# A hybrid attention and mixture-of-experts step on one core: identity products before the last expert products, a new order of work in the second layer, and token rows that wait in PSUM

## What is computed

```python
for l in range(2):
    h = adaln(x, norm_mix[l], shift, scale)          # RMS norm, then scale and shift
    x = x + gate * (attention(h @ w_in[l]) @ w_out[l])
    h = adaln(x, norm_ffn[l], shift_f, scale_f)
    x = x + gate_f * moe(h)                          # 16 experts, top 2 of one group
# moe: scores = softmax(h @ w_router); two experts a token
#      hid = silu(h @ w_gate[e]) * (h @ w_up[e]);  out = sum_e gates[e] * (hid @ w_down[e])
```

## Time and profile before

| | us |
|---|---|
| median of 3 runs (lowest, highest) | 1244.72 (1243.37, 1246.33) |
| the profiled execution, its whole time | 1242.9 |
| its span, first to last instruction | 1241.1 |
| PE busy | 1164.1 |
| DVE busy | 279.8 |
| ACT busy | 187.7 |

### The profile page before, as it was taken

How to read it: one execution, slowest core, us unless ns; L and a number is a source line. 1 busy time by engine, 2 the same in 40 slices (tenths; PEclk the granted TensorE clock), 3 DMA queues, 4 the chain that set the end, 5 groups by cost and what they waited for, 6 DMA issues and landing times.

```text
span 1241.1 us, 13752 instructions
## 1 busy us (share of the span) xinstructions
PE 1164.1 (94%) x5533; PEld 515.1 (42%) x5533; DVE 279.8 (23%) x673; ACT 187.7 (15%) x441; POOL 56.4 (5%) x68
## 2 busy tenths in 40 slices
PE   4999999999988899899999999999999998989898
PEld 1445464443423233334344454753434434343333
DVE  1146533121010101021232354312021110202013
ACT  1224322010000000001021343210001100000010
POOL 0412000000000000000013020000000000000000
PEclk9999999999999999999999999999999999999999
DMA  9999999999999999999997559899999999999997
GB/s 375 383 383 375 414 423 429 424 431 427 429 427 427 429 429 428 429 427 429 420 392 259 203 196 397 339 391 413 426 428 428 428 428 428 428 430 428 427 425 296
DMA packets 60084, 494.18 MB, mean 398 GB/s; under 512 B 5490, under 2 KB 6658, under 8 KB 28420
## 3 DMA queue, kind: packets, MB, share of 16 engines
q1 hardware_dynamic: 56992, 485.88, 94.5%
q0 software_dynamic: 2864, 7.46, 1.9%
q10 hardware_dynamic: 180, 0.17, 0.0%
HBM read 490.72 MB, written 3.16 MB: 398 GB/s over the span
## 4 chain that ended last, share of the span: by engine, by line
PE 72%; DMA 24%; issue 2%; ACT 1%; SPq 1%; DVE 1%; POOL 0%; DVEq 0%
PE bank L1190 39%; PE bank L942 12%; DMA ring<-in_w_up 9%; DMA ring<-in_w_gate 7%; DMA ring<-in_w_down 6%; PE bank L952 3%; PE bank L1140 3%; PE bank L898 3%; PE bank L1151 3%; DMA ring<-in_w_in_ab 2%; PE bank L874 2%; PE bank L1216 1%; PE bank L959 1%; PE bank L997 1%; PE bank L1246 1%
## 5 line engine op out<-in xcount | busy, mean ns | idle before, releaser
L1190 PE MATMUL bank<-ring,hT 128*64 128x512 f32 x2520 | 574.3, 606 | 48.0 <-issue 20.1
L1190 PEld LDWEIGHTS bank<-ring,hT 128*64 128x64 f32 x2520 | 191.2, 139 | 401.6 <-issue 392.8
L942 PE MATMUL bank<-ring,hT 128*128 128x512 f32 x320 | 141.8, 600 | 3.1 <-DMA ring<-in_w_in_ab 2.4
L942 PEld LDWEIGHTS bank<-ring,hT 128*128 128x128 f32 x320 | 60.5, 192 | 79.9 <-issue 77.3
L1983 DVE TENSOR_TENSOR work<-work,bank 128x512 f32<-128x512 f32 x56 | 38.5, 688 | 164.0 <-PE bank L1151 163.8
L1976 DVE TENSOR_TENSOR work<-work,bank 128x512 f32<-128x512 f32 x32 | 22.0, 688 | 223.6 <-PE bank L1190 198.8
L1190 PE MATMUL bank<-work,hT 128*64 128x512 f32 x284 | 69.5, 593 | 0.0
L1140 PE MATMUL bank<-work 128*128 128x128 f32 x512 | 60.3, 275 | 0.0
L1140 PEld LDWEIGHTS bank<-work 128*128 128x128 f32 x512 | 58.7, 192 | 1.6 <-issue 1.6
L1519 ACT ACTIVATE hT<-bank 128x512 f32<-128x512 f32 x32 | 19.0, 595 | 256.9 <-PE bank L1246 256.9
L2024 DVE COPY work<-bank 128x512 f32<-128x512 f32 x14 | 9.7, 692 | 207.3 <-PE bank L1190 207.3
(11 more groups left out here) (220 smaller groups left out, 754.4 us busy)
## 6 DMA issues: line engine op xcount, KB each, us to landing
ring<-in_w_gate SPq DMA_DIRECT2D x56, 2048.0 KB, 17.7
ring<-in_w_up SPq DMA_DIRECT2D x50, 2048.0 KB, 17.2
ring<-in_w_down SPq DMA_DIRECT2D x46, 2048.0 KB, 17.0
ring<-in_w_mod SPq DMA_DIRECT2D x23, 2048.0 KB, 11.1
work<-in_w_up SPq DMA_DIRECT2D x8, 2048.0 KB, 15.2
ring<-in_w_down SPq DMA_DIRECT2D x14, 1024.0 KB, 14.7
ring<-in_w_in_c SPq DMA_DIRECT2D x6, 2048.0 KB, 21.1
ring<-in_w_in_ab SPq DMA_DIRECT2D x4, 2048.0 KB, 21.6
```

The source lines that it names most:

```text
L942: ins = pe.matmul(b[:, 0:n], hT[:, c, t * P:(t + 1) * P], w[:, c, 0:n], start=i == 0, stop=i == DC - 1)
L1190: ins = pe.matmul(bank[banks[j]][64 * e:64 * e + 64, :], lhs[:, 4 * h + c, 64 * e:64 * e + 64], weights(e, c, j), start=(h, c) == (0, 0), ...
```

## The change

It has these parts.

1. **Identity products.** In the last pair of each layer `rows_first` multiplies the four halves of `x` by the identity into the banks of the last scatter, four products of 128 x 512, after the down unit 8 and before unit 10. The last scatter adds to them. `add_last` on DVE is gone: in layer 0 DVE copies the four halves out (`rows_out`), and ACT squares the sample halves straight from PSUM; in layer 1 ACT copies all four.
2. **`shift_logits(1)`** moves from between the scatter products of layer 0 to just before `rows_first`.
3. **Order of DVE and of the first projection** at the start of layer 1: both gated halves of t = 0 come before the norm, whose request is split in two; the first projection of layer 1 begins with chunk 0 (ACT's) instead of chunk 4.
4. **Order of the dense units of layer 1**: `("in", 4, 0)` directly after `("in", 4, 1)`; `("mod", 1, 2, 0)` and `("in", 5, 1)` after the scores of batch 2; values wait only for the unit that they read.
5. **Token rows of layer 1**: the sample's transposes (`hk`, 1) no longer stand before the output projection, but one half after `xT` and one after `("hT", 1, 0)`. `keep_busy(2)` after `xT` and its wait go, `keep_busy(5)` becomes 2.
6. **Parked rows.** In layer 1 ACT copies the four halves of `x` to banks 4 to 7 before and during the first gather (`park`), and DVE copies them back after the last down product of pair 0. So in pair 0 the hidden transposes go to banks 0 and 3, the down products to 0 and 1, and the gather of pair 1 to 2 and 1. PE waits for the count job before the first gather.
7. **A megabyte into x.** `load_where_parked` loads row block 2 of the last down unit of pair 0, 0.5 MB for each expert, into `x`, once the rows are parked and before `load_halves(0, ...)`, which loses its two loads of 0.5 MB.

```diff
-        "scores": [("in", 4, 1), ("in", 5, 1)],
-        0: [("in", 4, 0)],
-        1: [("T", 0), ("mod", 1, 2, 0), ("in", 5, 0)],
+        "scores": [("in", 4, 1), ("in", 4, 0)],
+        0: [("mod", 1, 2, 0), ("in", 5, 1)],
+        1: [("T", 0), ("in", 5, 0)],
         2: [("mod", 1, 2, 1)],
         3: [("mod", 1, 2, 2)],
         4: [("wo", 0, 1)],
         5: [("wo", 1, 1)],
         (6,): [("mod", 1, 2, 3)],
         (7,): [("modT", 2)],
-        7: [("hT", 1, 1), ("wo", 0, 0), ("hk", 1), ("woh", 0), ("woh", 1), ("rt", 1), ("xT",),
-            ("rt", 0), ("hT", 1, 0), ("hk", 0), ("pos",)]}}
+        7: [("hT", 1, 1), ("wo", 0, 0), ("woh", 0), ("woh", 1), ("rt", 1), ("xT",), ("hkh", 1, 0),
+            ("rt", 0), ("hT", 1, 0), ("hkh", 1, 1), ("hk", 0), ("pos",)]}}
...
-                    for half in range(2):
+                    for half in range(2 if n else 1):
...
+                def load_where_parked(e):
+
+                    slot = moe_slot(l, ring_turn(0, MOE_UNITS - 2 + e))
+                    src = a["w_down"][l].rearrange("e k n -> (e k n)")[e * D * D:(e + 1) * D * D].rearrange("(h p r) -> h p r", h=2, p=P)[1]
+                    sp.wait_ge(m["parked"], 2 if e else 4)
+                    sp.wait_ge(moe_ld[l][slot], 16)
+                    sp.dma_start(x[:, e, :], src[:, 2 * D:3 * D]).then_inc(moe_ld[l][slot], 16)
...
                     load_quarter(1)
+                    load_where_parked(1)
+                    load_where_parked(0)
                     load_halves(0, MOE_UNITS - 2, 1)
                     load_halves(1, 0, 2)
...
-                    keep_busy(5)
+                    keep_busy(2)
...
-                    c = 4 * ((i + 1) % 2) + i // 2
+                    half = (i + 1 + l) % 2
+                    c = 4 * half + i // 2
...
-                if j % BATCHES == 0:
-                    pe.wait_ge(*emptied_by(("qkv", l, IN_UNITS[l] - 1, t)))
+                if l == 0 and j % BATCHES == 0:
+                    pe.wait_ge(*emptied_by(("qkv", 0, 4, t)))
+                elif l == 1 and b % 2 == 0:
+                    pe.wait_ge(*emptied_by(("qkv", 1, 4 + b // 2, t)))
...
-                if l == 1:
-                    pe.wait_ge(mod_emptied, 6)
-                    keep_busy(2)
...
+                    apart = bank[3] if l else bank_of(("hT", l, 1, 0, 0))
...
+                    if first and l:
+                        pe.wait_ge(*emptied_by(("count", 1)))
...
+                        if l == 1 and early and (n, k) == (0, SLOTS + 2) and j:
+                            pe.wait_ge(m["hg_ready"], 4)
+                        if l == 1 and early and (n, k) == (1, 0):
+                            pe.wait_ge(m[f"yd{j}_ready"], 1)
...
+                def rows_first(n):
+
+                    pe.wait_ge(m["y_added"], 4 * n + 5)
+                    for t in (1, 0):
+                        for h in range(2):
+                            pe.matmul(last_bank(t, h)[:, :], K("ident"), x[:, t, h * UC:(h + 1) * UC], start=True, stop=False)
+
                 def last_scatter():
 
                     for t in (1, 0):
                         for h in range(2):
                             pe.wait_ge(m["yd_gated"], 3 - 2 * t + h)
                             pe.matmul(last_bank(t, h)[:, :], GT[:, t, :], ydg[t][:, h * UC:(h + 1) * UC],
-                                      start=True, stop=True).then_inc(m["scattered"], 1)
-                        if (l, t) == (0, 1):
-                            shift_logits(1)
...
+                        if l == 0:
+                            shift_logits(1)
+                        rows_first(n)
                         last_product(n, 10, (6, 7), hidT, m["down_half"])
...
+                        down = (0, 1) if isinstance(n, int) and (l, n) == (1, 0) else (6, 7)
+                        product(n, 8, down, hidT, m["ht_ready"])
+                        product(n, 10, down, hidT, m["ht_ready"], m["down_half"])
...
+                def park(t, u):
+
+                    act.wait_ge(*emptied_by({(0, 0): ("hT", 1, 1, 0, 0), (0, 1): ("hT", 1, 1, 0, 1), (1, 0): ("hk", 1, 1, 1), (1, 1): ("hk", 1, 0, 0)}[t, u]))
+                    act.activation(bank[4 + 2 * t + u][:, :], x[:, t, u * UC:(u + 1) * UC], ACT.Copy).then_inc(m["parked"], 1)
...
+                if l:
+                    park(1, 0)
+                    park(1, 1)
+                    park(0, 0)
                 gathered(0)
...
+                end = more * PAIRS + PAIRS
+                if l == 0:
+                    for u in range(2):
+                        act.wait_ge(m["scattered"], 4 * end + u + 1)
+                        act.activation(xn(0, 1)[:, u * UC:(u + 1) * UC], last_bank(1, u)[:, :], ACT.Square,
+                                       accum_out=ss[:, 1 + 4 * u:2 + 4 * u]).then_inc(half_squares if u == 0 else ssq_ready, 1)
+                else:
+                    for t in (1, 0):
+                        for u in range(2):
+                            act.wait_ge(m["scattered"], 4 * end + 2 * (1 - t) + u + 1)
+                            act.activation(x[:, t, u * UC:(u + 1) * UC], last_bank(t, u)[:, :], ACT.Copy).then_inc(x_ready, 1)
...
+                    if first and l:
+                        dve.wait_ge(moe_used[l], used(0, 11))
+                        for t in (1, 0):
+                            for u in range(2):
+                                dve.tensor_copy(x[:, t, u * UC:(u + 1) * UC], bank[4 + 2 * t + u][:, :]).then_inc(m["y_added"], 1)
...
-                    add_last(end, 1, 0)
-                    add_last(end, 1, 1)
                     gate_down(0, 0)
-                    norm_asked(1, 0, 1)
                     gate_down(0, 1)
+                    first_half_scaled(1, 0, 1)
+                    rows_out(end, 1, 0)
+                    second_half_asked(1, 0, 1)
+                    rows_out(end, 1, 1)
+                    dve.wait_ge(x_ready, 4 + 2)
                     normed_rows(1, 0, 1)
-                    add_last(end, 0, 0)
+                    rows_out(end, 0, 0)
                     modulate(1, 0, 1)
-                    add_last(end, 0, 1)
+                    rows_out(end, 0, 1)
```

More of the change, by code:

```diff
@@ L1060, in logits, with token_rows @@
                     keep_busy(2)
-            def token_rows(l, t):
-                for h in range(2):
+            def token_rows(l, t, halves=(0, 1)):
+                for h in halves:
                     if (l, t, h) == (1, 0, 1):
@@ L1138, in gather @@
                                 at = (4 * h + c) * P
-                                to = bank_of(("hT", l, 1, 0, 0)) if first and h == 0 and c >= 2 else bank[2 if first and h else h]
+                                to = apart if first and h == 0 and c >= 2 else bank[2 if first and h or parked and not h else h]
                                 ins = pe.matmul(to[:, c * P:(c + 1) * P], htok(t)[:, at:at + P], pick[:, t, :],
@@ L1237, in last_scatter @@
                             pe.matmul(last_bank(t, h)[:, :], GT[:, t, :], ydg[t][:, h * UC:(h + 1) * UC],
-                                      start=True, stop=True).then_inc(m["scattered"], 1)
-                        if (l, t) == (0, 1):
-                            shift_logits(1)
+                                      start=False, stop=True).then_inc(m["scattered"], 1)
                 def hidden_transposed(n, h):
                     pe.wait_ge(m["hid_done"], 2 * n + h + 1)
+                    to = bank[3 * h if isinstance(n, int) and (l, n) == (1, 0) else 4 + h]
                     for c in range(4):
-                        ins = pe.transpose(bank[4 + h][:, c * P:(c + 1) * P], quarter(hid, h, c), K("ident"))
+                        ins = pe.transpose(to[:, c * P:(c + 1) * P], quarter(hid, h, c), K("ident"))
                     ins.then_inc(m["ht_done"], 1)
@@ L1518, in hidden_transposed @@
                     act.wait_ge(m["ht_done"], 2 * n + h + 1)
-                    act.activation(hidT[:, 4 * h:4 * h + 4, :], bank[4 + h][:, :].rearrange("p (c s) -> p c s", c=4),
+                    at = bank[3 * h if isinstance(n, int) and (l, n) == (1, 0) else 4 + h]
+                    act.activation(hidT[:, 4 * h:4 * h + 4, :], at[:, :].rearrange("p (c s) -> p c s", c=4),
                                    ACT.Copy).then_inc(m["ht_ready"], 1)
@@ L1545, in pair @@
                         act.wait_ge(moe_used[l], used(n, 11))
-                        act.activation(yd[:, UC:2 * UC], bank[7][:, :], ACT.Copy).then_inc(m["yd1_ready"], 1)
+                        act.activation(yd[:, UC:2 * UC], bank[1 if isinstance(n, int) and (l, n) == (1, 0) else 7][:, :], ACT.Copy).then_inc(m["yd1_ready"], 1)
+                if l:
+                    park(1, 0)
+                    park(1, 1)
+                    park(0, 0)
                 gathered(0)
@@ L1578, in _ @@
                     router(l, 1)
+                    token_rows(l, 1, (0,))
                 router(l, 0)
@@ L1582, in _ @@
                     mod(1, 1)
```

(5 more changed lines are left out.)

58 lines of the change are left out of this document (36 added, 22 removed).

## The result

The changed kernel takes 1247.53 us (median of 15 runs, 1246.59 to 1250.38), the one before 1243.80 (15 runs, 1242.37 to 1246.76). The ratio is 1.0029, its 95% interval 1.0023 to 1.0036: 0.3% slower, outside the 0.2% that a measurement can't tell from nothing. The profiled execution has a span of 1245.1 us against 1241.1, so +4.0.

A forecast was written before the change was run, and what follows sets the result against it. Experts were taken as bound by weight loads, layer 1's dense part by PE, whose delay until 813 us moves the end. 3.03 - 0.78 + 2.18 - 0.06 = +4.37 us on 1244.72 gave 1249.1, range 1243.0 to 1251.5.

The forecast's parts named there:

- the sum: Whole kernel, all terms added: +4.37 us, 1249.1 us, own range 1247.5 to 1250.3, chance 53%.
- Price of an identity product: Ahead of down unit 10 in both layers: four identity products take 3.6 us, 1.8 as lower end.
- The rival of 1.8 us or less: Identity products cheap, like transposes or faster: 1245.5 us at 1.8 for four, 1244.2 at 0.9; chance 13%.
- Cover of 1.42 us and no more: PE's wait before unit 10 covers 1.42 us; unit 10 comes 3.88 us later in layer 0, 2.18 in layer 1.
- Gain behind unit 10: After unit 10: 0.85 us sooner in layer 0 (0.4 scaling, 0.45 first projection), 0.06 in layer 1.
- slow clock: Rival: PE's clock falls when idle at layer 1's start, or a new wait opens: +1.7, 1250.8 us; chance 13%.
- Order of the dense part: Dense units of layer 1: same products, earlier loads not waited for, cost 0; up to about 1 us if waits opened.
- Token rows: Before layer 1's experts: transposes off the output projection chain, 0.88 us sooner, about +0.1 for the count wait, -0.78 together.
- PE's delay moves every later load: Between 632 and 813 us, each microsecond PE loses or gains moves every later load and the end equally.
- Parked rows: Pair 0 of layer 1: copies stay behind PE's work, cost 0, or 1 us if an order of waits is worse.
- Megabyte: Loads around 802 to 813 us: the DMA hole only moves, gain 0, upper bound 2.45; rival that it counts, 12%.
- First gather to 8b of layer 1: From layer 1's first gather to the second piece of its down unit 8: difference of 0 predicted.

The follow-up runs named there:

- e2: Changed kernel with every identity product made twice, the first result overwritten by the second: 1254.84 us, ratio 1.0090 to the kernel before.
- e1: Changed kernel without identity products in both layers, DVE adding as before and in its old order at layer 0's end: 1243.25 us, ratio 0.9998 to the kernel before.
- e3: Changed kernel with modulation unit (1, 2, 0) back between the prompt's transposed heads and input unit 5: 1247.10 us, ratio 1.0025 to the kernel before.
- e7: Changed kernel without identity products, DVE's old order at layer 0's end, modulation unit back, shift_logits behind up unit 6: 1242.85 us, ratio 0.9989 to the kernel before.
- e8: Changed kernel with the sample's token rows transposed before the output projection again, keep_busy and its wait as before: 1247.82 us, ratio 1.0027 to the kernel before.
- e9: The kernel of e7 with the parked rows and the megabyte undone as well: 1242.17 us, ratio 0.9991 to the kernel before.
- e10: The same kernel as e7, measured again: 1242.65 us, ratio 0.9989 to the kernel before.
- e4: Changed kernel, rows still parked, but the megabyte loaded into the ring after the first halves as before: 1248.87 us, ratio 1.0045 to the kernel before.
- e6: The same kernel as e4, measured again beside the changed kernel: 1249.22 us, ratio 1.0036 to the kernel before.
- e5: The changed kernel itself, unaltered, measured again: 1248.07 us, ratio 1.0033 to the kernel before.

## Why the prediction was right

1249.1 us was forecast, 1247.5 measured; the likeliest case, the sum, came true, though at the lower edge of its own range (1247.5 to 1250.3). The gap of 1.6 us has two parts. The kernel before came out at 1243.8 with more runs and not at 1244.7, which is 0.9; the rest is in the sum, +4.4 forecast and +3.7 in the medians (+4.0 in the span).

- **Price of an identity product**: 3.6 us for four forecast, 3.68 and 3.70 measured, 7.11 for eight in e2. The rival of 1.8 us or less is out. So, for this float32 data, is the time by the rule of the Trainium skill ("TensorE: Matmul & The Clock Gate", section "Wait — 56ns, not 53.3ns?") of 215.7 ns from product to product: the trace disagrees, with 16 instructions in 7.11 us, 444 ns each, two to a product.
- **Cover of 1.42 us and no more**: unit 10 starts 9.00 us after 8b against 5.07, +3.93 in layer 0 (forecast 3.88), and 7.21 against 5.07, +2.14 in layer 1 (forecast 2.18). e1 brings the wait back, e2 shows the full price without it.
- **Gain behind unit 10**: 0.85 forecast in layer 0, 1.18 measured (unit 10 to first projection, 14.14 to 12.96); 0.06 forecast in layer 1, 0.34 measured (14.16 to 13.82). Both were taken too small, which makes up 0.6 us of the sum. In layer 0 the square of the second half started where forecast (2.05 us after the end of unit 10), but the scaling 3.71 us after it and not 4.0, and the transposes followed 0.81 us later where it was 0.96 before; the first projection followed them 0.29 us sooner than before, where 0.45 was forecast for ACT's chunk. In layer 1 ACT's last copy ends 11.39 us after unit 10 starts, against 11.50 for DVE's last addition before; the rest of the 0.34 lies behind it. The pauses ahead of the transposes (0.79) and the first projection (0.26) brought no slow clock: the granted clock is 1.00 in the windows of 10 us from 620 to 660, with PE busy 9.10 of 10 us from 640 to 650.
- **Order of the dense part**: this step was wrong. It was costed at 0 because nothing waited for the loads and the products are the same. e3 shows 1.00 us (0.67 where the identity products are out, e1 against e7). What was overlooked is that the modulation product also stood between ACT's exponentials and the next use of their bank. The prediction had "up to about 1 us" as a bound, but for a wait for transposed heads or shared scores, and not for a bank that is still being read.
- **Token rows**: -0.78 forecast, of it -0.88 for the transposes, for which e8 shows -0.81, and +0.1 for the count, for which e9 shows 0.01 to 0.11.
- **PE's delay moves every later load**: this holds. In e2 the first gather starts at 805.56, 7.37 us later than before, and from there to 8b it takes 423.01 us, within the range of the others: the delay is carried in full.
- **Parked rows**: 0 forecast. The marks of pair 0 and pair 1 are all 2.99 us later, the same as the first gather. PE's next wait for loads begins 175.93 us after the first gather, in the kernel before 175.92; and e9 against e7 and e10 shows no difference.
- **Megabyte**: 0 forecast with the hole moving. It moved, from 804 to 814, in the windows of e4 and of the change. In the times e4 and e6 leave up to about 2 us open; e9 against e7 and e10 comes out at 0.3 us, with intervals of over 1 us to each side and for megabyte and parking together. So that it is worth nothing rests on the windows and on the unmoved issue of the next loads, and the times leave about 1 us open.
- **First gather to 8b of layer 1**: -0.79 was not forecast. It isn't a gain of the change. The same stretch takes from 422.70 to 425.29 us in the other kernels, without order by their edits; e5, the same program as the change, has 424.40. There PE waits 1.46 us before 8b where the first profile has 0.58. The stretch before the first 8b drifts as well, from 619.91 to 623.18 us in the kernels whose edits all lie behind it. So one execution's span hides some 2 us of such drift, and that the sum met it within 0.4 us is partly luck: for the dense part and token rows together 1.2 us too little was forecast; on the other side stand 0.6 us of gain behind unit 10 that was not forecast and 0.8 of drift.

## What to carry to other kernels

Work put on the bound engine ahead of the last operands' product is free only up to the wait that stands there; take the wait's length from the timeline, subtract it once, and charge the rest in full. An independent unit between two uses of a bank is cover for whoever reads the bank, even if nothing waits for its own result; before moving it, look who is reading at that moment on the other engines. Bytes moved early count only if the queue doesn't run dry afterwards: find the first later load that waits for room, and ask whether it would be issued sooner.

## What was not expected of the hardware

ACT's copy of 128 x 512 values costs about the same in either direction. Three from SBUF into PSUM took 1.71 us and three from PSUM into SBUF 1.61 us, in the changed kernel's ACT timeline:

```profile
798.26 1.61 ACT L1437 ACTIVATE work<-bank 128x512 f32<-128x512 f32 x3
799.69 1.71 ACT L1542 ACTIVATE bank<-x 128x512 f32<-128x512 f32 x3
```

And the stretch from the first gather to 8b differs by 1.5 us between two executions of the changed kernel (422.89 and 424.40) and by 2.6 us over all the kernels run, at a mean granted clock of 0.985 to 0.989 over the whole execution. The drift lies almost wholly behind PE's first wait for loads in the expert pairs, in the changed kernel's PE timeline

```profile
978.57 7.09 PE L1215 MATMUL bank<-ring,hT 128*64 128x512 f32 x32 [1.46 <-issue]
```

From the first gather to the start of this wait it takes 175.93 us in the changed kernel and 176.06 in e5; from there to 8b, where PE waits again and again for weights, 246.96 and 248.34. What makes the loads themselves take longer in one execution than in another stays open.
